# Two transformer stacks on one core: the pass from one step to the next, rebuilt at every boundary

## The reference, cut to what matters

```python
x = x + 0.5 * swiglu(rmsnorm(x, ffn1_norm[i]), ffn1_w_gu[i], ffn1_w_down[i])
h = rmsnorm(x, mix_norm[i])
x = x + mixer(h)
x = x + 0.5 * swiglu(rmsnorm(x, ffn2_norm[i]), ffn2_w_gu[i], ffn2_w_down[i])
# second stack: modulate(x) = rms_norm(x, g) * (1 + scale) + shift, and gate * (...) on the way back
```

## Time and profile before

| | us |
|---|---|
| median of 3 runs | 3950.04 (3946.04 to 3951.96) |
| the profiled execution | 3948.77 |
| its span | 3946.8 |
| TensorE busy | 3787.2 |
| DVE busy | 2262.5 |
| ACT busy | 1286.1 |
| mean granted clock of TensorE | 0.984 |

### The profile page before, as it was taken

One profiled execution on the slowest core, in us unless ns is written; L12 is line 12 of the kernel. 1 busy time (PEld: TensorE's weight loads), 2 busy tenths in 40 slices (PEclk: granted clock), 3 DMA queues, 4 the chain that ended last, 5 costly groups with the idle time before them and its releaser, 6 DMA issues.

```text
span 3946.8 us, 59688 instructions
## 1 busy us (share of the span) xinstructions
PE 3787.2 (96%) x24380; PEld 3394.2 (86%) x24380; DVE 2262.5 (57%) x3345; ACT 1286.1 (33%) x1760; POOL 257.5 (7%) x322
## 2 busy tenths in 40 slices
PE   6998999999999999999998998999999999999999
PEld 6987889998799985999987798998989599998598
DVE  5754568781477765787745477555533555551255
ACT  3322133331333334333322233434311343431143
POOL 0000300000000001000002200000000200000000
PEclk9999999999999999999998999999999999999999
DMA  7651066674376743666721265563512255463443
GB/s 255 229 166 62 30 218 235 210 240 133 131 241 212 240 169 123 240 234 219 233 90 68 74 221 187 183 211 133 200 61 75 88 185 197 153 199 120 154 168 106
DMA packets 453525, 660.42 MB, mean 167 GB/s; under 512 B 15288, under 2 KB 385299, under 8 KB 452904
## 3 DMA queue, kind: packets, MB, share of 16 engines
q1 hardware_dynamic: 432280, 579.48, 43.0%
q0 software_dynamic: 21072, 78.56, 6.1%
HBM read 656.94 MB, written 2.00 MB: 167 GB/s over the span
## 4 chain that ended last, share of the span: by engine, by line
PE 93%; DVE 3%; ACT 1%; issue 1%; DMA 1%; SPq 0%; POOL 0%; POOLq 0%; ACTq 0%; DVEq 0%
PE ps L570 14%; PE ps L572 14%; PE ps L571 14%; PE ps L588 6%; PE ps L589 6%; PE ps L590 6%; PE ps L949 4%; PE ps L779 4%; PE ps L2571 3%; PE ps L972 2%; PE ps L428 1%; PE ps L1127 1%; PE ps L2289 1%; PE ps L1478 1%; PE ps L2292 1%; PE ps L1049 1%
## 5 line engine op out<-in xcount | busy, mean ns | idle before, releaser
L570 PE MATMUL ps<-parts 128*128 128x256 f32 x4576 | 1303.1, 285 | 6.4 <-DVE parts L689 6.4
L571 PE MATMUL ps<-parts 128*128 128x256 f32 x4576 | 1295.6, 283 | 0.0
L572 PE MATMUL ps<-parts 128*128 128x256 f32 x4576 | 1295.5, 283 | 0.0
L570 PEld LDWEIGHTS ps<-parts 128*128 128x128 f32 x4576 | 877.7, 192 | 13.4 <-issue 7.2
L571 PEld LDWEIGHTS ps<-parts 128*128 128x128 f32 x4576 | 877.8, 192 | 6.2
L572 PEld LDWEIGHTS ps<-parts 128*128 128x128 f32 x4576 | 877.7, 192 | 0.0
L512 DVE TENSOR_TENSOR parts<-ring,parts 128x2048 fp32r<-128x2048 f32 x286 | 654.8, 2292 | 226.7 <-ACT parts L501 225.3
L638 ACT ACTIVATE silu<-ps 128x256 f32<-128x256 f32 x286 | 109.9, 384 | 1494.7 <-PE ps L572 1494.7
L501 ACT ACTIVATE parts<-ring 128x2048 fp32r<-128x2048 f32 x286 | 545.2, 1909 | 48.1 <-DMA ring<-in_ffn_w_out 43.1
L694 DVE TENSOR_TENSOR silu<-silu,ps 128x256 f32<-128x256 f32 x286 | 119.7, 418 | 603.3 <-ACT silu L638 603.3
L588 PE MATMUL ps<-parts 128*128 128x512 f32 x1144 | 449.3, 393 | 0.0
(11 more groups left out here) (422 smaller groups left out, 3919.3 us busy)
## 6 DMA issues: line engine op xcount, KB each, us to landing
ring<-in_ffn_w_gu SPq DMA_DIRECT2D x176, 1024.0 KB
ring<-in_ffn_w_in SPq DMA_DIRECT2D x110, 1024.0 KB
ring<-in_ffn_w_down SPq DMA_DIRECT2D x88, 1024.0 KB
ring<-in_ffn_w_out SPq DMA_DIRECT2D x55, 1024.0 KB
ring<-in_gdn_w_in SPq DMA_DIRECT2D x32, 1024.0 KB
arena<-in_w_mod POOLq DMA_DIRECT2D x24, 1024.0 KB, 5.6
xn<-in_w_mod POOLq DMA_DIRECT2D x24, 1024.0 KB, 5.6
arena<-in_w_mod POOLq DMA_DIRECT2D x48, 512.0 KB, 8.8
```

The lines of the kernel that those rows point to most:

```text
L570: nc.tensor.matmul(dst, w_u[:, m, :], h_hi[:, k, :], start=(k == 0), stop=False)
L571: nc.tensor.matmul(dst, w_u[:, m, :], h_lo[:, k, :], start=False, stop=False)
L572: ins = nc.tensor.matmul(dst, w_l[:, m, :], h_hi[:, k, :], start=False, stop=(k == KD - 1))
```

## The change

- **Early scaling.** `add_to_x` calls `scale_next` after each quarter. After the add of quarter 2 it scales row tile 0 for the next step. FFN 8's adds scale both tiles for FFN 9 (after quarters 0 and 1), and their gate's temporary becomes `silu` in place of `xn`. FFN 0 and FFN 8 have no early scaling.
- **Order on the engines.** `norm_dve` handles row tile by row tile: in an FFN the modulation and both lower parts of tile 0 stand ahead of the scaling of tile 1. In first-block steps ACT squares quarter 3 behind its copy of quarter 0.
- **Mixers' first tiles by row tile.** gdn and sb make the first two 256-column products as halves of 128 columns; dsa, sgu and even move a product of row tile 0 ahead of tile 1's transposes (`even` swaps its products 1 and 2). The gate's rows go between or behind the transposes, in banks 2 and 3 for the mixers, and their wait goes back.
- **Last three f-tiles by quarter.** Quarters 0 and 1 of tiles 19 and 20, then of tile 21, then quarters 2 and 3 of all three. The last turn of TensorE's loop is unrolled. `mod_pe` of the last tile now stands directly behind its up product.
- **No unread products**: `spin` is gone.
- Up products stay whole: the first waits for the second row tile's parts.

```diff
-        for q, (t, h, _) in enumerate(QUARTERS):
+    def norm_pe(pe, at, t, k=0):
+        for q in (2 * t, 2 * t + 1):
...
-            if q == 1:
-                spin(pe, 7)
...
+    def early_rows(at):
+        if at["kind"] == "ffn" and at["n"] in (0, CTX_FFN):
+            return ()
+        return (0, 1) if at["kind"] == "ffn" and at["n"] == CTX_FFN + 1 else (0,)
+
+    def scale_rows(dve, at, t, src=x_sb):
+        row = (at["kind"], at["n"]) in ROWED
+        if row:
+            dve.wait_ge(row_loaded, 16 * (row_use(at) + 1))
+        dve.wait_ge(rstd_ready, TT * at["norm"] + t + 1)
+        for h in range(2):
+            scale_dve(2 * t + h, src, row)
+
+    def scale_next(dve, at, q):
+        then = next_step(at)
+        if then["kind"] == "final":
+            return
+        if at["kind"] == "ffn" and at["n"] == CTX_FFN:
+            if q < TT:
+                scale_rows(dve, then, q)
+        elif q == 2:
+            scale_rows(dve, then, 0)
+
+    def norm_dve(dve, at, after, src=x_sb):
+        for t in range(TT):
+            if t not in early_rows(at):
+                scale_rows(dve, at, t, src)
+            after(t)
...
+    def norm_copy_act(act, at):
+        for q in range(NQ - 1):
+            square_act(act, at, q)
+        quarter_copy(act, at, 0)
+        square_act(act, at, NQ - 1)
+        quarter_copy(act, at, 2)
...
     def ffn_pe(pe, at):
-        norm_pe(pe, at)
-        if at["n"] >= 8:
-            gate_pe(pe, at)
-        else:
-            spin(pe, 0)
...
+        norm_pe(pe, at, 0)
+        if at["n"] == CTX_FFN + 1:
+            pe.wait_ge(ctx_ready, 2)
+        if at["n"] >= 8:
+            gate_pe(pe, at)
+        norm_pe(pe, at, 1)
+        up_free(0)
+        up_products(0, 0, T, row=1).then_inc(up_done, 1)
+        up(1)
...
-        with pe.Fori(0, ITERS) as it:
+        with pe.Fori(0, ITERS - 1) as it:
             for u in range(step):
                 up(tiles0 + u, it)
                 down(tiles0 + u - 2, it)
                 if at["n"] < 8:
                     mod_pe(pe, at, u, it)
+        for u in range(step):
+            i = NFT - step + u
+            up(i)
+            if i < NFT - 1:
+                down(i - 2)
+            if at["n"] < 8:
+                mod_pe(pe, at, u, ITERS - 1)
+
+        a, b, c = NFT - 3, NFT - 2, NFT - 1
+        pe.wait_ge(act_done, f0 + b + 1)
+        pe.wait_ge(down_lower, f0 + b + 1)
+        for q in range(2):
+            quarter(a, q, False, False)
+            quarter(b, q, False, False)
+        pe.wait_ge(act_done, f0 + c + 1)
+        pe.wait_ge(down_lower, f0 + c + 1)
+        for q in range(2):
+            quarter(c, q, False, True).then_inc(tail_done, 1)
+        for q in range(2, NQ):
+            quarter(a, q, False, False)
+            quarter(b, q, False, False)
+            ins = quarter(c, q, False, True)
+            ins.then_inc(*((tail_done, 1) if q < NQ - 1 else (down_done, 3)))
...
     def ffn_act(act, at):
         split_first_act(act, at)
-        norm_act(act, at, src=x_ctx if at["n"] == CTX_FFN else x_sb)
+        src = x_ctx if at["n"] == CTX_FFN else x_sb
+        for q in range(NQ - 1):
+            square_act(act, at, q, 0, src)
+        if at["n"] >= 8:
+            square_act(act, at, NQ - 1, 0, src)
         for q, (t, h, _) in enumerate(QUARTERS):
...
+            if q == 0 and at["n"] < 8:
+                square_act(act, at, NQ - 1)
...
+        def lower_rows(t):
+            if n >= 8:
+                modulate_dve(dve, at, 2 * t, *ffn_modulation(at))
+            for q in (2 * t, 2 * t + 1):
+                h = q % 2
+                dve.wait_ge(h_upper, NQ * at["ffn"] + q + 1)
+                part_ = (slice(None), slice(4 * h, 4 * h + 4), slice(t * P, (t + 1) * P))
+                nc.vector.tensor_tensor(h_lo[part_], turned_ps(q), h_hi[part_], ALU.subtract).then_inc(h_split, 1)
+
+        norm_dve(dve, at, lower_rows, x_ctx if n == CTX_FFN else x_sb)
...
+            if c == 0:
+                wait_h(pe, at, 0)
+                qkv(0, 0, P)
+                qkv(1, 0, P)
+                norm_pe(pe, at, 1)
+                wait_h(pe, at, 1)
+            qkv(c, P if c < 2 else 0, T).then_inc(gdn_qkv, 1)
...
+        wait_h(pe, at, 0)
         w_in(0, 0)
+        norm_pe(pe, at, 1)
+        wait_h(pe, at, 1)
         w_in(1, 0)
...
     def sgu_pe(pe, at):
-        norm_pe(pe, at)
-        gate_pe(pe, at)
-        gate_wait_pe(pe, at)
+        norm_pe(pe, at, 0)
         for n, (side, q, i) in enumerate(SGU):
+            if n == 1:
+                norm_pe(pe, at, 1)
+                gate_pe(pe, at)
             if n < TT:
-                pe.wait_ge(hT_ready, h_before(at) + n + 1)
-                pe.wait_ge(h_shifted, shifted_before(at) + n + 1)
+                wait_h(pe, at, n)
+            if n == 2:
+                gate_wait_pe(pe, at)
```

More of the change, by code:

```diff
@@ L303, in next_row_sp, with square_act @@
         row_load(sp, [a for a in PLACES if (a["kind"], a["n"]) == ROWED[n]][0])
-    def norm_act(act, at, k=0, src=x_sb):
[L307 to L312, removed]
-                else:
[L314 to L326, removed]
+    def square_act(act, at, q, k=0, src=x_sb):
+        n = at["norm"] + k
+        t, h, cols = QUARTERS[q]
+        if src is not x_sb:
+            if at["kind"] == "ffn":
+                act.wait_ge(ctx_loaded, 16)
+                act.wait_ge(x_ready, NQ * at["update"])
+            else:
+                act.wait_ge(ctx_ready, q + 1)
+                if at["update"]:
+                    act.wait_ge(x_ready, NQ * at["update"])
+        elif at["update"]:
+            act.wait_ge(x_ready, NQ * (at["update"] - 1) + q + 1)
+        else:
+            act.wait_ge(x_loaded, 16)
+        if n:
+            act.wait_ge(turned, NQ * n)
+        nc.scalar.activation(xn[:, t, cols], src[:, t, cols], ACT.Square, scale=float(D) ** -0.5,
+                             accum_out=sumsq[:, q:q + 1]).then_inc(sumsq_ready, 1)
+    def norm_act(act, at, k=0, src=x_sb):
+        for q in range(NQ):
+            square_act(act, at, q, k, src)
     def inv_sqrt(pool, dst, src, factor, eps):
@@ L349, in scale_dve @@
         ins.then_inc(xn_ready, 1)
-    def norm_row_dve(dve, at):
-        dve.wait_ge(row_loaded, 16 * (row_use(at) + 1))
+    def early_rows(at):
[19 more added lines that the diff above has]
+    def norm_dve(dve, at, after, src=x_sb):
         for t in range(TT):
[L355 to L359, removed]
+            if t not in early_rows(at):
+                scale_rows(dve, at, t, src)
+            after(t)
+    HT = {"ffn": 2, "gdn": 2, "sb": 2, "dsa": 2, "ctx": 0, "even": 2 + NQ, "sgu": 2, "final": 0}
     def h_before(at):
@@ L365, in shifted_before, with wait_h @@
     def shifted_before(at):
-        return 2 * sum((a["kind"], a["n"]) in GATES for a in PLACES[:PLACES.index(at)])
+        return 2 * sum(NORMS[a["kind"]] > 0 for a in PLACES[:PLACES.index(at)] if not (a["kind"] == "ffn" and a["n"] < 8))
+    def wait_h(pe, at, t):
+        pe.wait_ge(hT_ready, h_before(at) + t + 1)
+        pe.wait_ge(h_shifted, shifted_before(at) + t + 1)
     def turned_ps(q):
@@ L578, in down, with quarter @@
             pe.wait_ge(down_lower, count(f + 1, it, step))
[L579 to L585 removed]
+            for q in range(NQ):
+                ins = quarter(i, q, first, False)
+            ins.then_inc(down_done, 1)
+        def quarter(i, q, first, last):
+            t, h, cols = QUARTERS[q]
+            f = f0 + i
+            w_u, w_l = down_hi[:, f % UPB, :], down_lo[:, f % UPB, :]
             tokens, dst = slice(t * P, (t + 1) * P), ps[:, q, :]
@@ L1464, in sb_pe, with qk @@
     def sb_pe(pe, at):
-        norm_pe(pe, at)
-        pe.wait_ge(hT_ready, h_before(at) + NQ)
+        norm_pe(pe, at, 0)
+        def qk(c, a, b):
+            w = part(at["load"] + c // 6, c // 2 % 3).rearrange("p (k c) -> p k c", k=KD)
+            for k in range(KD):
+                ins = nc.tensor.matmul(ps[:, c % 4, a:b], w[:, k, (c % 2) * P:(c % 2 + 1) * P], hT[:, k, a:b],
+                                       start=(k == 0), stop=(k == KD - 1))
+            return ins
         for q in range(12):
@@ L1476, in sb_pe @@
                         pe.wait_ge(sb_qks, c - 3)
[L1477 to L1480 removed]
+                    qk(c, P if q == 0 else 0, T).then_inc(sb_qk, 1)
                 else:
```

209 lines of the change are left out of this document (96 added, 113 removed).

## The result

Before the change the median of 11 runs is 3950.57 us (3944.89 to 3957.03); after it the median of 11 runs is 3958.31 us (3956.28 to 3963.53). The ratio is 1.0023, with a 95% interval from 1.0014 to 1.0033: slower, by 7.7 us. The prediction was 3949, with 3939 to 3958 as its range; the result lies just outside it, at rival C's 3960.

The account below looks back on a forecast made before the run. TensorE, busy 96% of the span, was taken as the bound. Shorter mixer, FFN 9, even and sgu starts nearly cancelled against clock falls and serial order elsewhere: -0.8 us in sum, 3949 us forecast, range 3939 to 3958.

Parts of the forecast that it names:

- rival C: FFN starts: every clock fall is followed by a second, so first up products run slow; +10.6 us, 3960; chance 0.15.
- The chains: Summed serial work from L, the tail's last record's end, to a step's first product; 6.3 us in first-block FFNs.
- DVE forms both lower parts before it scales tile 1: First-block FFN starts: this order puts tile 1's scaling behind tile 0's lower parts, its first half ending at L+4.1 us.
- the price of the fall at the seven first-block passes: FFN passes from a tail: slow clock costs 1.2 us, against 0.8 gained; net +0.4 each, +2.8 together.
- FFN 10 to 12: Second-block FFN starts: later tile 1 scaling and clock falls cost +2.6, +3.1 and +1.6 us, together +7.3.
- The serial order: Second-block FFN starts: tile 1 is scaled only after tile 0's lower parts; +1.2 us at FFN 11.
- The mixers: gdn twice, sb and dsa: tile 0's products run while tile 1 is prepared; -2.4 us each, -9.6 together.
- even: Start of even: same parts as sgu, but a second slow stretch was already paid before; -2.4 us taken.
- the start, FFN 0 and FFN 8: Starts without early scaling feel only the new order and slower clock; +3.8 us together.
- The wait for the modulation's last step: Three FFN-to-FFN passes: column sums directly behind the last up product wait 0.2 us for DVE; +0.6 together.
- The 0.8 us by which first-block passes were to become shorter: First-block FFN starts: the new order brings the first up product 0.8 us earlier, before any clock fall.
- Rival B: Whole kernel: the clock holds despite the new idle gaps; sum -22.6 us, 3927; chance 0.13.

Follow-up runs that it names:

- run 10: Changed kernel with unread products in both idle places of every FFN start, plus tile 1 scaled earlier in every FFN: 3922.43 us, 0.9939 of before.
- run 1: Changed kernel with both fillers: unread products between the two tiles' transposes and behind tile 1's at every FFN start; 3923.20 us, 0.9932 of before.
- run 2: Kernel before the change without its two batches of unread products, nothing else: 3951.27 us, 1.0005 of before.
- run 9: Changed kernel with unread products only behind tile 1's transposes at FFN starts, none in the gap between tiles: 3943.72 us, 0.9986 of before.
- run 4: Changed kernel with unread products in both idle places of FFN starts and tile 1 scaled earlier in FFN 8 to 12: 3921.93 us, 0.9932 of before.
- run 8: Changed kernel with tile 1's transposes ahead of the first products in gdn, sb and dsa: 3968.75 us, 1.0050 of before.
- run 3: Changed kernel, no fillers, with tile 1 scaled ahead of both lower parts of tile 0 in FFN 8 to 12: 3949.33 us, 0.9998 of before.
- run 7: Changed kernel with the tail (last two f-tiles by quarter) and full hardware loop of before: 3963.23 us, 1.0038 of before.
- run 5: Changed kernel with unread products in both idle places, but only in FFN 0 to 7: 3937.81 us, 0.9968 of before.
- run 6: Changed kernel with unread products only in the gap between the two tiles' transposes, at every FFN: 3937.79 us, 0.9969 of before.

## Why the prediction was wrong

**The chains were right.** First up product of an FFN from a tail: predicted L+6.3 by the sum and 0.8 earlier than before, measured L+5.8 to 6.4; with the clock held the passes took 0.8 to 1.2 less than before (column "both fillers"). FFN 9: predicted 9.4, measured 9.48. FFN 11: 11.6 and 11.8. gdn: 1.8 and 1.77. TensorE's gap ahead of tile 1 was 2.60 to 2.78 us and not 3.1. The step "DVE forms both lower parts before it scales tile 1" was right in its time, but it isn't the reason alone: run 10 shows rstd ready at the same moment.

**The step that failed is the price of the fall at the seven first-block passes.** The prediction expected a fall at each, rightly, but took one stretch of low clock, 1.7 us lost, and laid it at even steps behind the gap: 1.2 us each, with 0 and 2.2 as bounds. In after the low clock of FFN 2 lasted some 6.8 us, 3.4 of them lost, and 5.3 of the 6.8 lay on up products. It costs 2.3 us a pass by run 1, 2.0 by run 2. Six of the seven passes came to +1.3 or +1.4 instead of +0.4, the seventh (FFN 6) to -0.1; together +8.2 where +2.8 stood, 5.4 us. This is rival C, "every fall is followed by a second one", which the prediction had at 0.15 and whose deciding point was 2.2.

So it was the number of stretches that was wrong, and not what one costs. Where only one came, in run 9, six passes lost 1.0 to 1.4 us to it and ended at +0.1 to +0.4, as forecast, and FFN 6 of after lost 0.9. The low clock begins under the transposes of tile 1 (1.78 us long), and between them and the up products TensorE stands still again; unless products fill that place (run 9), it mostly stays low under the first up products.

**FFN 10 to 12** came to +9.8 instead of +7.3, the same error: the clock of FFN 10 is down over all three windows shown above (0.62, 0.50, 0.60), and the second has 1.10 us of work in it. The serial order itself was priced at 1.2 a pass; run 4 finds 0.7 to 0.9 where the clock holds.

**The mixers** gave -2.6 at dsa, near the -2.4 predicted, and -1.5 at sb (-2.8 with both fillers); their rearrangement is worth 2.6 each on average by run 8, a fall avoided included. But gdn 1 took 3.4 us more than before, 5.8 more than predicted, the largest miss of a single step. Its start is in order (first product at L+1.93); the loss is inside, in a body that the change doesn't touch. The windows of after over its middle and end, and the middle in before:

```profile
2050.00:2160.00 110.00, 92.81 (x489) 83.84 (x488) 52.75 (x72) 26.10 (x53) 21.74 (x18) 0.84 0.21 73
2160.00:2264.00 104.00, 96.78 (x658) 80.34 (x656) 53.28 (x69) 26.81 (x43) 26.23 (x25) 0.98 0.10 33
```
```profile
2050.00:2160.00 110.00, 92.88 (x525) 84.20 (x524) 55.13 (x74) 27.30 (x56) 23.63 (x20) 0.89 0.21 74
```

0.84 against 0.89 over 110 us is 5.5 us more of lost clock, part of it under idle time. It isn't the scatter of one execution: gdn 1 took 3.4, 4.1, 4.4 and 3.0 more than before in runs 3, 7, 8 and 9, where first-block passes still have falls, and -1.9 in each of runs 1, 5 and 6, where they have none (-3.3 and 0.0 in runs 4 and 10, 7.6 more in before without unread products). The prediction had no term for falls inside a step that isn't changed. gdn 0 doesn't follow that pattern (-1.7 in after, +1.6 with both fillers), so why a body catches more falls at one time than at another stays open: no run moved it alone.

Between the profiles the miss is 13.2 us: 5.4 at the first-block FFNs, 5.8 at gdn 1, 2.5 at FFN 10 to 12, and -0.5 for all the rest together. Between the medians it is 8.5; how that divides isn't known.

**The rest.** even gave 3.6 (2.4 predicted), FFN 9 2.0 (2.8), the start, FFN 0 and FFN 8 cost 2.5 (3.8), sgu gave 0.1 (0.5). The wait for the modulation's last step is there and has its size: DVE's step ends at 705.57 and the column sums start at 705.63, where the up products, 0.12 apart, had their last start at 705.33: 0.2 us. The 0.8 us by which first-block passes were to become shorter came out, but not from where the prediction had them: it gave them to the new order and held the unread products to cost nothing beside it, and run 2 gives 0.7 to the unread products and leaves 0.3 for the order. Rival B's time, 3927, is near what the kernel does when the clock is made to hold (3923), though its parts came out otherwise: the mixers -5.7 where it had -9.6, even -9.8 where it had -5.

In after an idle time of 2.60 us, with transposes on both sides, goes with a fall at FFN 2, and filling it ended the falls at all seven passes. Whether it is the idle time alone, or the transposes around it too, no run separates. The Trainium skill ("TensorE: Matmul & The Clock Gate", section "HAM oscillation — how this bites in real kernels") would have let such a gap pass, as the prediction said; the traces disagree with it here too, and it was right that the prediction's sum did not go by it.

## What to carry to other kernels

Before you shorten a chain on the engine that bounds the kernel, ask what that engine does in the gaps that you open: here each first-block FFN pass became 0.8 to 1.2 us shorter, and most then paid 2.3 us because the clock fell around a gap of 2.6 to 2.8. Price a fall at the work that stands behind it, in whole stretches and with a second one if more idle time follows, not at an average. And don't remove unread work as waste until you know what it holds up; put it where the engine stands still, where it costs nothing, not where the next real product waits behind it.

## What the runs showed of the hardware

- The clock fell from 2.4 to 1.2 GHz around an idle time of 2.60 us that lay between transposes; with that time filled, an idle time of 0.84 us behind the transposes brought no fall. The idle time alone doesn't decide: at FFN 5 it was 2.78 us both in after, which fell, and in run 9, which didn't, and in before without unread products FFN 2 fell and FFN 6 didn't, with the same waits ahead of their transposes (1.44 and 0.94 us).
- Work behind a fall shortens it: 8 filler records in 1.46 us between the transposes and the up products did not prevent the fall at FFN 2 (0.74), but the clock stood at 0.83 in the next four microseconds instead of 0.50.
- TensorE's busy time hides a fall: the window 721 to 725 reads 4.00 of 4.00 us both in after at half clock and in the filled kernel at full clock. The number of instructions in it (21 against 35) tells them apart.
- Untouched code changes its time with the falls that it happens to catch: gdn 1, whose body no run altered, took between 3.3 us less and 7.6 us more than before, of which its changed start explains some 2 us at the lower end; in its middle (110 us) the clock was 0.84 in after and 0.89 in before.
